# One-hots of the first key for every fourth group made by ScalarE, and a Sqrt moved into the stage that follows

## The reference

```python
def chunk(zc):                              # 128 tokens at a time, so two halves
    q = (zc @ peer_wq).reshape(128, 8, 2, 128)
    s1, s2 = q[:, :, 0] . keys1, q[:, :, 1] . keys2       # 128 scores per head and half
    v1, i1 = top_k(s1, 16);  v2, i2 = top_k(s2, 16)
    top_s, top_pos = top_k(v1[:, None] + v2[None, :], 16)
    expert = i1 * 128 + i2                  # at the chosen positions: 16 of 16384 experts per head
    gate = softmax(top_s)
    act = gelu(sum_d peer_u[expert] * zc)
    w = gate * act
    return sum over the 8 * 16 chosen experts of w * peer_v[expert]
```

## Time and profile before

| | us |
|---|---|
| median of 3 executions | 2675.05 |
| lowest and highest of them | 2673.89 and 2683.71 |
| profiled execution, its own time | 2678.4 |
| its span in the trace | 2676.6 |
| from the copy of `turned` (t = 1) to the end of the last `add_row` in the trace | 2223.94 to 2280.98 |

### The profile page before, as it was taken

How to read it: one execution, slowest core, us unless ns; L and a number is a source line. 1 busy time by engine, 2 the same in 40 slices (tenths; PEclk the granted TensorE clock), 3 DMA queues, 4 the chain that set the end, 5 groups by cost and what they waited for, 6 DMA issues and landing times.

```text
span 2676.6 us, 32030 instructions
## 1 busy us (share of the span) xinstructions
PE 2255.0 (84%) x11484; PEld 1810.4 (68%) x11484; DVE 2114.4 (79%) x2971; ACT 1063.5 (40%) x1637; POOL 696.4 (26%) x834
## 2 busy tenths in 40 slices
PE   8999989999999999989999964444555558999998
PEld 7997778888888888879888831111222325777776
DVE  6986647665566556577766999989999989899997
ACT  5433554443444344453542110000345534544443
POOL 1000000000000000000001353533444442889884
PEclk9999999999999999999999976556677778999999
DMA  6534345555555555545558999999999995999996
GB/s 226 183 124 109 114 154 165 187 186 189 184 188 188 188 188 180 165 130 169 176 171 353 421 420 420 419 420 420 420 416 412 418 418 183 363 390 409 403 396 261
DMA packets 314374, 730.97 MB, mean 273 GB/s; under 512 B 21025, under 2 KB 223009, under 8 KB 275745
## 3 DMA queue, kind: packets, MB, share of 16 engines
q0 software_dynamic: 73728, 402.69, 37.1%
q1 hardware_dynamic: 240402, 325.99, 35.9%
q10 hardware_dynamic: 144, 1.05, 0.1%
HBM read 727.57 MB, written 2.10 MB: 273 GB/s over the span
## 4 chain that ended last, share of the span: by engine, by line
DVE 23%; PE 16%; DMA 12%; issue 4%; POOL 3%; ACT 1%; DVEq 0%; PEldq 0%; ACTq 0%; POOLq 0%
DVE row L2502 12%; DMA row<-in_peer_u,expert 8%; DMA row<-in_peer_v_rows,expert 4%; PE pl L866 4%; DVE pl L2518 4%; PE pl L873 3%; PE pg L1295 2%; POOL row L802 2%; PE pl L1260 1%; PE pl L869 1%; PE pl L870 1%; PE pg L1286 1%; PE pl L1189 1%; POOL spread_lo L777 1%; DMA v_tile<-in_peer_v_dense 1%
## 5 line engine op out<-in xcount | busy, mean ns | idle before, releaser
L1962 DVE TENSOR_TENSOR wlo<-raw,whi 128x1024 fp32r<-128x1024 f32 (+1 forms) x436 | 517.8, 1208 | 374.9 <-ACT whi L1352 373.1
L1352 ACT ACTIVATE whi<-raw 128x1024 fp32r<-128x1024 f32 (+1 forms) x436 | 444.5, 1039 | 412.1 <-PE pl L873 407.5
L2502 DVE CUSTOM_DVE_ANT_0 row<-row,pg 128x2048 f32<-128x2048 f32 x256 | 574.6, 2284 | 33.9 <-DMA row<-in_peer_u,expert 31.7
L1260 PE MATMUL pl<-row,diag 128*128 128x512 f32 x404 | 315.6, 927 | 334.4 <-DMA row<-in_peer_v_rows,expert 296.1
L866 PE MATMUL pl<-x_split,whi 128*128 128x512 f32 x1888 | 478.6, 395 | 10.0 <-DVE x_split L1970 5.2
L1260 PEld LDWEIGHTS pl<-row,diag 128*128 128x128 f32 x404 | 101.4, 277 | 499.9 <-issue 437.0
L866 PEld LDWEIGHTS pl<-x_split,whi 128*128 128x128 f32 x1888 | 341.4, 190 | 74.5 <-issue 7.5
L873 PE MATMUL pl<-x_split,wlo 128*128 128x256 f32 x2656 | 373.6, 284 | 3.9 <-DVE wlo L1962 3.9
L873 PEld LDWEIGHTS pl<-x_split,wlo 128*128 128x128 f32 x2656 | 358.8, 192 | 23.2 <-DVE wlo L1962 4.5
L802 POOL DMA_INDIRECT row<-in_peer_v_rows,expert x256 | 305.3, 1193 | 170.0 <-DVE dots L2502 66.8
L802 POOL DMA_INDIRECT row<-in_peer_u,expert x256 | 242.0, 945 | 367.2 <-DVE dots L2502 156.1
(11 more groups left out here) (349 smaller groups left out, 2950.3 us busy)
## 6 DMA issues: line engine op xcount, KB each, us to landing
v_tile<-in_peer_v_dense SPq DMA_DIRECT2D x128, 512.0 KB
raw<-in_w_in SPq DMA_DIRECT2D x51, 1024.0 KB
raw<-in_w_gate SPq DMA_DIRECT2D x44, 1024.0 KB
raw<-in_w_up SPq DMA_DIRECT2D x44, 1024.0 KB
raw<-in_w_out SPq DMA_DIRECT2D x32, 1024.0 KB
raw<-in_w_down SPq DMA_DIRECT2D x32, 1024.0 KB
wq<-in_peer_wq SPq DMA_DIRECT2D x15, 1024.0 KB, 11.5
raw<-in_w_down SPq DMA_DIRECT2D x16, 768.0 KB
```

The source lines that it names most:

```text
L1260: last = mm(pl_all[:, c:c + width], diag[:, (at - 1) % 4, :], row[b][:, c - DENSE:c - DENSE + width], start=at == 1, stop=at == ADDED_ROWS ...
L1352: return nc.scalar.activation(o, i, ACT.Copy)
L1962: V.tensor_tensor(wlo[:, n % 4, 0:k, :], w[:, :, f, :], whi[:, n % 4, 0:k, :].bitcast(F32), ALU.subtract)\
L2502: V.tensor_tensor_reduce(row[b][:], row[b][:], z_tok[:], 1.0, 0.0, ALU.mult, ALU.add, dots[:, at:at + 1])\
```

## The change

In the spread stage, for the groups with g % 4 == 3 (3, 7, 11, 15, 19, 23, 27, 31) DVE no longer makes `hot_a`. ACT makes it in `second_first_keys`, by the first two of the three steps of `first_keys`, behind the diagonal (where the turn has one) and just ahead of the copy of the group before: at g = 2 it makes `hot_a` for group 3 and then copies group 2, and so on. At g = 30 `high_tile(0)` comes ahead of it. PE waits for `first_ready` in these eight groups as well. The Sqrt on one column goes from ahead of tile 1 to behind `high_weights(8)`.

```diff
@@ -1276,6 +1276,8 @@
                 pe.wait_ge(hot_ready, n + 1)
                 if t == 0:
                     pe.wait_ge(first_ready, FIRST_READY + 3 * n + 3)
+                elif g % 4 == 3:
+                    pe.wait_ge(first_ready, FIRST_READY + 3 * GROUPS + 2 * (g // 4) + 2)
                 banks = pg[0:3] if t else pl[0:2]
@@ -1844,6 +1846,18 @@
                     last = activation(a[:, c, :], a[:, c, :], ACT.Copy, scale=turned[:, 2, token:token + 1])
                 last.then_inc(first_ready, 1)
 
+            def second_first_keys(g):
+
+                n = GROUPS + g
+                act.wait_ge(hot_used, n - HOTS + 1)
+                a = hot_a[n % HOTS]
+                for c in range(GROUP):
+                    token = g * GROUP + c
+                    last = activation(a[:, c, :], iota[:], ACT.Abs, scale=-1.0, bias=turned[:, 0, token:token + 1])
+                last.then_inc(first_ready, 1)
+                act.wait_ge(first_ready, FIRST_READY + 3 * GROUPS + 2 * (g // 4) + 1)
+                activation(a[:], a[:], ACT.Relu, scale=-1.0, bias=ones[:, 0:1]).then_inc(first_ready, 1)
+
             u = 0
             for table, t, n, k in ROW_ORDER[:LATER]:
                 if table == "v":
@@ -1887,10 +1901,13 @@
                     weight_matrix(*ROW_ORDER[LATER + at + 2][1:])
                 if g == GROUPS - 2:
                     high_tile(0)
+                if (g + 1) % 4 == 3:
+                    if g == 2:
+                        act.wait_ge(turned_ready, 2)
+                    second_first_keys(g + 1)
                 spread_copy(1, g)
             act.wait_ge(spread_ready, TT * GROUPS)
             high_weights(0)
-            activation(small[:, 60:61], halfpi[:], ACT.Sqrt)
 
@@ -1900,6 +1917,8 @@
             for m in range(1, NKEY):
                 high_tile(m)
                 high_weights(m)
+                if m == 8:
+                    activation(small[:, 60:61], halfpi[:], ACT.Sqrt)
                 if m == NKEY // 2:
@@ -2535,7 +2554,7 @@
                 full = [P, GROUP, NKEY]
-                if t:
+                if t and g % 4 != 3:
                     V.tensor_tensor(a[:], iota[:].unsqueeze(1).broadcast_to(full),
```

## The result

The changed kernel takes 2684.75 us, the median of 22 executions, and the kernel before 2678.38, also of 22. The ratio is 1.0024, with a 95% interval of 1.0017 to 1.0030: 6.4 us slower, a quarter of a percent, and clear of no change. The profiled executions have spans of 2683.2 and 2676.6 us, 6.6 apart, so the two traces can be set side by side. (Lines up to 1278 keep their numbers; line 1286 is now 1288, 1295 is 1297, 1352 is 1354, 2518 is 2537, 2539 is 2558, 2547 is 2566 and 2653 is 2672.)

The account below looks back on a forecast made before the run. PE was taken to bound the spread stage. Keys +6.4 us (waits 5.4, restarts 1.0) less 0.9 for the Sqrt made +5.5, taking the median from 2675.05 to 2680.6; range 2671 to 2688 (8 in 10).

Parts of the forecast that it names:

- PE bounds the spread stage, DVE's relief is worth 0: Spread stage: PE's stream has no gap, so the 4.9 us taken off DVE is hidden and gains 0.
- The near tie of 1.63 and 1.64 us: Spread stage: DVE starts a group every 1.63 us and PE's mean is 1.64, with DVE just ahead.
- The rival in which DVE paces the stage: Spread stage: DVE sets the pace, so its 4.9 us and the Sqrt's 0.9 come off, giving 2669; chance 0.07.
- ACT has the key ready about 0.6 us too late: Spread stage: PE waits for ACT's key 0.47 us at group 3, 0.60 at six groups, 1.34 at group 31; sum 5.4.
- A restart of PE costs 0.13: Spread stage: each wait empties PE's pipeline, costing 0.13 us more, eight times, 1.0 us together.
- Sum of the keys, +6.4: Spread stage: PE's waits of 5.4 us and restarts of 1.0 us together add 6.4 us; bounds 0 and 10.
- The Sqrt gains 0.9: Dense stage, tile 1: moving the Sqrt removes DVE's wait of 0.91 us for ACT; gain 0.9, bounds 0 and 1.3.
- the full transfers take it back: Dense stage: lower bound of the Sqrt's gain, 0, if the full transfers use up the time saved.
- The clock falls: Spread stage: rival in which PE's waits bring its clock back to 1.2 GHz, doubling the time of work; chance 0.06.
- the 8 us or 50 us: Spread stage: about 8 us of PE's full-rate work at the low clock gives 2689; low throughout the stage, +50.
- If the keys are hidden: Spread stage: rival in which PE's slack or ACT's overlap hides the keys, leaving only the Sqrt, 2674; chance 0.12.
- The signs: Profile after: eight PE waits on ACT, spread stage 6 to 7 us longer, DVE idle some 10, chain alternating PE and ACT.

Follow-up runs that it names:

- e8_tile_at_5: The changed kernel with ACT's copy of tile 0 moved from turn 30 to turn 5; one execution, spread stage 54.91 us.
- e5_every_second: The changed kernel with ACT making the first keys of every odd group from 3 on, fifteen in all; ratio to the kernel before 1.0054.
- e2_sqrt_only: The kernel before with only the Sqrt moved, to behind the weights of tile 8; ratio to the kernel before 0.9996.
- keys only: The changed kernel with the Sqrt back in its old place ahead of tile 1; ratio to the kernel before 1.0034.
- e3_relief_only: The kernel before without the first keys of groups 3, 7, ... 31, made by neither DVE nor ACT; ratio to the kernel before 0.9998.
- e10_before_98: The kernel before with 98 in place of 101 rows added by PE, 11 in the spread stage; ratio to the kernel before 1.0013.
- e9_early_98: The changed kernel with keys one turn earlier, tile 0 copied at turn 7, and 98 in place of 101 rows added by PE; ratio to the kernel before 1.0002.

## Why the prediction was right

It forecast no measurable change with a slower sign, +5.5 us on the three executions known then; measured are +6.4, within 0.5%. With 22 executions of each the slower sign is measurable. The time itself, 2684.75, lies 4 us above the 2680.6 that was forecast, and 3.3 of them because the median of the kernel before moved from 2675.05 to 2678.38 with more executions. By its steps:

- *PE bounds the spread stage, DVE's relief is worth 0.* Shown: without those eight instructions, and with nobody making these keys, the stage keeps its length. The near tie of 1.63 and 1.64 us was rightly read by who waits, not by who is busier. The rival in which DVE paces the stage became true only with three `add_row` less.
- *ACT has the key ready about 0.6 us too late.* Forecast were waits of 0.6 for six groups, 1.34 for the last and 0.47 for the first; the gaps are 0.59 to 0.68, 1.33 and none. That the last one was long because of the copy of tile 0 is shown by moving it (0.39).
- *A restart of PE costs 0.13.* This term was mis-sized. The interval between the `add_row` around group 7 grew from 4.39 to 5.31 us, so 0.92 for a gap of 0.67; around group 11 it grew by 0.84 for a gap of 0.61. A restart costs 0.24. I had taken the 0.10 by which the first four matmuls of 512 columns last longer after a wait, and 0.03 for the signal. Left out was the overlap of PE's pieces: in the timeline an `add_row` is 1.88 us long and the next piece starts 1.72 after it, so 0.16 before its modelled end (more than the tenth of a microsecond stated ahead of the rows). Behind a gap there is no such overlap, and the first eight records last 1.13 in place of 1.05: 0.16 + 0.08 = 0.24. The width of the matmuls is not the reason. By the same measure the restart with 512 columns in the earlier trace rows costs 0.27: 0.16 of overlap, and 1.04 us to the next piece (2295.62 to 2296.66) in place of 0.93.
- *Sum of the keys, +6.4.* The stage grew by 6.93. By the intervals between the `add_row`, group 3 cost 0.12 where 0.60 was forecast, the six in the middle 0.87 on average where it was 0.73, the last 1.57 where it was 1.47: -0.5, +0.9 and +0.1. The two errors partly cancel, and that is luck: where the front was quick (`e8_tile_at_5`), group 3 cost 0.82, and with it the sum would have been 7.6. The measured +6.4 lies below the stage's growth, though the Sqrt gained nothing that can be seen; its interval, 4.5 to 8.0 us, is too wide to read anything from that.
- *The Sqrt gains 0.9.* It gains nothing that can be seen; the lower bound, "the full transfers take it back", held, and it is the transfer of tile 2. At its new place it costs ACT only time that it would have waited. The Trainium skill's rule in "ScalarE: Activation LUTs" ("What ACT_TABLE_LOAD costs"), by which the move would have given up to 2.7, found no support: the table load took 1.28 us, as the page has it, but no drain shows beside it. The Sqrt on one column, 0.20 long, starts 0.01 us after the load, wherever the two stood.
- *The clock falls.* It did not, with gaps of up to 1.33 us: the stage behind its front is at 1.00. But such a fall is real, and far smaller than the 8 us or 50 us that I had weighed: in the kernel with a key in every second group it fell once, after a gap of 2.10 us, and cost 1.3. The Trainium skill's case in "TensorE: Matmul & The Clock Gate" ("A second HAM failure mode: psum-queue depth-cycling"), where frequent short idles between groups make the clock swing, is not borne out: seven such idles in the changed kernel moved it not at all, and fourteen in `e5_every_second` once.
- *"If the keys are hidden" had 0.12.* They were not, but one turn earlier they are.
- *The signs.* The waits came in seven of the eight places, the stage grew by 6.9 us, and the dense stage kept its length within 0.4. DVE idled 13.9 us in 56.79, where I had said some 10, for before it idled 3.0 in 50 already. The chain did not alternate between PE and ACT as printed, since the profile puts these waits down to "issue" or to DVE.

## What to carry to other kernels

Two engines that are 100% and 94% busy in a stage are not both its bound: follow the chain, and see which of them has the work ready when the other asks for it. Work taken from the one that waits is worth nothing, until the pacing engine has less to do too. And where work is given to an engine that has a third of its time free, its place in that engine's order counts more than its length: here the same instructions cost 7 us directly ahead of their use and 0 one turn earlier.

## What the runs showed of the hardware

The clock at the front of the stage differs from profile to profile, for the same work. The first three groups, 24 matmul records from the first to the end of the third, in `e2_sqrt_only` and in `e5_every_second`, whose first three groups are the same work:

```profile
2226.47 5.49 PE L1286 MATMUL pg<-hot_b,hot_a 128*128 128x128 f32 x24 [2.39 <-DVE hot_b L2548]
```

```profile
2222.57 4.63 PE L1288 MATMUL pg<-hot_b,hot_a 128*128 128x128 f32 x24 [2.39 <-DVE hot_b L2566]
```

5.49 us where the clock stood at the lower level (0.50 of full speed, 1.2 GHz) before the first matmul already and stayed there through all three. In the other it stood at 1.00 through the idle 2.39 us, fell to 0.50 within half a microsecond of the first matmul, and was back at 1.00 before the third group ended: 4.63. This hides or shows the first of PE's waits. Where the front was slow, ACT had the key of group 3 (nearly) in time, and the next interval was 3.62 and 3.81 us (changed kernel, keys only), no more than the 3.80 and 3.90 of `e3_relief_only` and `e2_sqrt_only`, which have no such key. Where it was quick, it was 4.32 and 4.38 (`e8_tile_at_5`, `e5_every_second`), against 3.50 in the kernel before. So the stage of one profile can't be compared with another's to better than about a microsecond, unless the front is read apart.

A wait of about two microseconds in a busy stretch lets the clock fall in some cases and not in others. It fell to 0.50 behind the 2.10 us ahead of group 9 in `e5_every_second`, and behind 2.47 us in the early dense stage of `e10_before_98`:

```profile
2292.97 2.08 PE L1295 MATMUL pg<-v_lo,spread_hi 128*128 128x512 f32 x4 [2.47 <-DVE v_lo L2653]
```

From 2293 to 2296 the granted clock is 0.50 there, and these matmuls take 2.08 us where others of their kind take 1.09. It stayed at 1.00 behind the 2.10 us ahead of group 25 in the first of these kernels, behind 2.18 us in the dense stage of `e9_early_98` and behind the 2.00 us of the earlier trace rows. What decides between them no run here shows. Behind none of the gaps of up to 1.35 us in the stage did it fall.
